# Letting the weights stand and the tokens move in the gate, up, gated-convolution and second query/key projections

## What is computed

```
# first block
h = rms_norm(x, attn_norm);  x = x + mixer1(h) @ w_out
h = rms_norm(x, ffn_norm);   x = x + (silu(h @ w_gate) * (h @ w_up)) @ w_down          # 2048 -> 5632 -> 2048
# second block; sh, sc, g come from silu(c) @ ada_w + ada_b
h = rms_norm(x, mix_pre_g) * (1 + sc1) + sh1
proj = h @ w_in                       # q, k, v (8 heads of 128 each), a, g (1024 each)
u = conv(a * sigmoid(g));  u = silu(layer_norm(u))                 # depthwise, 31 taps
y = concat(attention(q, k, v), u) @ w_out;   x = x + g1 * rms_norm(y, mix_post_g)
h = rms_norm(x, ffn_pre_g) * (1 + sc2) + sh2
y = (silu(h @ w_gate) * (h @ w_up)) @ w_down;   x = x + g2 * rms_norm(y, ffn_post_g)
```

## Time and profile before

| | |
|---|---|
| median of 3 runs | 2319.97 us (2319.22 to 2321.0) |
| the profiled execution | 2319.94 us |
| its span | 2318.0 us |
| TensorE busy, weight loads busy | 98%, 81% of the span |
| VectorE, ScalarE, GpSimd busy | 65%, 47%, 8% |
| HBM | 508.04 MB read, 220 GB/s over the span |

### The profile page before, as it was taken

How to read it: one execution, slowest core, us unless ns; L and a number is a source line. 1 busy time by engine, 2 the same in 40 slices (tenths; PEclk the granted TensorE clock), 3 DMA queues, 4 the chain that set the end, 5 groups by cost and what they waited for, 6 DMA issues and landing times.

```text
span 2318.0 us, 29331 instructions
## 1 busy us (share of the span) xinstructions
PE 2264.0 (98%) x10348; PEld 1870.6 (81%) x10348; DVE 1516.0 (65%) x1956; ACT 1086.5 (47%) x1515; POOL 174.3 (8%) x194
## 2 busy tenths in 40 slices
PE   8999999999999999999999999989999999999998
PEld 6888877888888888888878887777888888888886
DVE  5445476767777777777776886776777544554545
ACT  5565453544434444344445775544443344444444
POOL 5000100000000000000001885000000000000000
PEclk9999999999999999999999999999999999999999
DMA  7556507678888888888766664575888666666654
GB/s 222 177 177 195 160 28 278 228 254 283 276 280 282 279 276 277 288 279 276 260 228 191 192 185 122 210 262 180 278 276 269 190 190 189 191 190 195 190 179 150
DMA packets 274503, 511.79 MB, mean 221 GB/s; under 512 B 20071, under 2 KB 28949, under 8 KB 274124
## 3 DMA queue, kind: packets, MB, share of 16 engines
q1 hardware_dynamic: 270252, 509.94, 69.4%
q10 hardware_dynamic: 4128, 0.26, 0.1%
HBM read 508.04 MB, written 2.10 MB: 220 GB/s over the span
## 4 chain that ended last, share of the span: by engine, by line
PE 93%; DVE 2%; issue 1%; ACT 1%; DMA 1%; SPq 0%; DVEq 0%; ACTq 0%
PE bank L945 30%; PE bank L961 28%; PE bank L962 28%; DMA raw<-in_w_out 1%; PE bank L916 1%; PE bank L1018 1%; PE bank L1090 1%; PE bank L930 1%; PE bank L1006 1%; ACT w_hi L1381 0%; DVE ada_acc L1770 0%; PE bank L1059 0%; PE bank L818 0%; PE bank L1047 0%; PE bank L1009 0%
## 5 line engine op out<-in xcount | busy, mean ns | idle before, releaser
L1793 DVE TENSOR_TENSOR w_lo<-raw,w_hi 128x1024 fp32r<-128x1024 f32 x760 | 936.9, 1236 | 598.8 <-ACT w_hi L1381 591.2
L1381 ACT ACTIVATE w_hi<-raw 128x1024 fp32r<-128x1024 f32 x760 | 802.3, 1059 | 976.3 <-PE bank L945 930.4
L961 PE MATMUL bank<-w_hi,act_hi 128*128 128x512 f32 x2016 | 793.2, 393 | 3.6 <-DVE act_lo L1583 3.6
L962 PE MATMUL bank<-w_hi,act_lo 128*128 128x512 f32 x2016 | 786.5, 390 | 0.0
L945 PE MATMUL bank<-w_lo,act_hi 128*128 128x512 f32 x2080 | 558.1, 390 | 0.0
L945 PEld LDWEIGHTS bank<-w_lo,act_hi 128*128 128x128 f32 x2080 | 391.5, 188 | 82.5
L961 PEld LDWEIGHTS bank<-w_hi,act_hi 128*128 128x128 f32 x2016 | 379.6, 188 | 82.2 <-DVE act_lo L1583 4.2
L962 PEld LDWEIGHTS bank<-w_hi,act_lo 128*128 128x128 f32 x2016 | 379.7, 188 | 78.0 <-issue 0.7
L961 PE MATMUL bank<-w_hi,mid_hi 128*128 128x512 f32 x960 | 380.1, 396 | 11.8 <-ACT w_hi L1381 8.6
L962 PE MATMUL bank<-w_hi,mid_lo 128*128 128x512 f32 x960 | 375.4, 391 | 0.0
L1770 DVE SCALAR_TENSOR_TENSOR ada_acc<-ada_raw,c_act,ada_acc 128x512 f32<-128x512 f32 x360 | 269.7, 749 | 7.7 <-DMA ada_raw<-in_ada_w 0.5
(11 more groups left out here) (269 smaller groups left out, 1009.1 us busy)
## 6 DMA issues: line engine op xcount, KB each, us to landing
ada_raw<-in_ada_w SPq DMA_DIRECT2D x192, 512.0 KB, 5.2
raw<-in_w_gate SPq DMA_DIRECT2D x176, 512.0 KB, 4.4
raw<-in_w_up SPq DMA_DIRECT2D x176, 512.0 KB, 4.5
raw<-in_w_down SPq DMA_DIRECT2D x176, 512.0 KB, 4.4
raw<-in_w_in SPq DMA_DIRECT2D x168, 512.0 KB, 3.9
raw<-in_w_out SPq DMA_DIRECT2D x64, 512.0 KB, 5.5
raw<-in_cmp_w_k SPq DMA_DIRECT2D x4, 512.0 KB, 4.5
raw<-in_cmp_w_v SPq DMA_DIRECT2D x4, 512.0 KB, 4.5
```

Of the source, the lines that this page charges most:

```text
L961: pe.matmul(A_[t][:, :], h_, w_hi[:, s, kk, :], start=(k == 0), stop=False)
L962: pe.matmul(A_[t][:, :], l_, w_hi[:, s, kk, :], start=False, stop=False)
L1381: act.activation(w_hi[:, U % SPLIT_SLOTS].rearrange("p k n -> p (k n)"), raw[:, R % RAW_SLOTS].rearrange("p k n -> p (k n)"), ACT.Copy).th ...
L1793: dve.tensor_tensor(w_lo[:, U % SPLIT_SLOTS].rearrange("p k n -> p (k n)"), raw[:, R % RAW_SLOTS].rearrange("p k n -> p (k n)"), w_hi[:, U ...
```

## The change

For gate and up of both feed-forwards, and in the second input projection for a, g, queries and keys (the kinds `gate`, `up`, `keep_a`, `glu` and the `plain` ones of the second block; `across(C)` says which), a block of 128 rows by 128 weight columns is the stationary operand and the 256 tokens move. The result comes out turned, so the transposes and the copies behind them go. A unit becomes eight row blocks by 128 columns, except in the first chunk of a stage (`WHOLE`), which keeps the shape of the old unit because its inputs arrive block by block; its banks are first cleared with a product by zero. Tokens now lie along the free dimension, so the reciprocal root of the first feed-forward's norm can no longer be a scale per partition: it is spread to all partitions by one product (`rs_row`), VectorE multiplies the gate by it before Silu, and for up it is left out and applied where the down result is added to x. `mid_hi` and `mid_lo` are made from `zsb`. The value projections, the first stage, output and down chunks stay as they were.

```diff
+    WHOLE = (S_FFN1[0]["C"], S_IN2[0]["C"], S_FFN2[0]["C"])
+    KH = KPU * CW // P
...
-    TURNS = [c for _, c in IN1 if c[0] != "value"] + [c for _, c in IN2 if c[0] not in ("value", "keep_a")]
+    TURNS = [c for _, c in IN1 if c[0] != "value"]
+    DIRECT = [c for _, c in IN2 if c[0] == "plain"]
+    ACROSS = ("gate", "up", "keep_a", "glu")
+    def across(C):
+        p = consumer_of[C]
+        return p[0] in ACROSS or p in DIRECT
...
+                    if across(c["C"]) and c["C"] not in WHOLE:
+                        k, n0 = KH * (u % 2), at(c["n0"] + P * (u // 2), r, c["n_step"])
+                        sp.dma_start(raw[:, R % RAW_SLOTS].rearrange("p a n -> p (a n)").rearrange(
+                            "p (k n) -> p k n", n=P), W[c["w"]][:, k:k + KH, bass.ds(n0, P)]).then_inc(
+                            raw_loaded[R % RAW_SLOTS], 16)
...
-                if prev[0] == "up":
-                    q = prev[1]
-                    pe.wait_ge(h_ready, at(2 * q + 2, r, 2))
-                    if q >= 1:
-                        pe.wait_ge(mid_lo_done, at(2 * q, r, 2))
-                    for t in range(TT):
-                        for c in range(HPC):
-                            ins = pe.transpose(TURN[t][:, c * P:(c + 1) * P], zsb[:, t, c * P:(c + 1) * P], ident[:, :])
-                        ins.then_inc(h_turned, 1)
...
+                if across(c["C"]):
+                    whole = c["C"] in WHOLE
+                    part_of = list(itertools.product(range(KPU), range(HPC))) if whole else list(range(KH))
+                    def block(m, a, w, stop=False):
+                        if whole:
+                            kk, j = m
+                            k, lhsT = KPU * u + kk, w[:, s, kk, j * P:(j + 1) * P]
+                        else:
+                            j, k = u // 2, KH * (u % 2) + m
+                            lhsT = w[:, s].rearrange("p k n -> p (k n)")[:, m * P:(m + 1) * P]
+                        return pe.matmul(A_[j // 2][:, j % 2 * T:(j % 2 + 1) * T], lhsT, a[:, k, :],
+                                         start=(not whole and k == 0 and a is hi and w is w_hi),
+                                         stop=(stop and k == KD - 1 and not (whole and j % 2 == 0)))
+                    pe.wait_ge(hi_done, at(U + 1, r, 2 * nu))
+                    if whole and u == 0:
+                        pe.wait_ge(zero_made, 1)
+                        for b in range(2):
+                            pe.matmul(A_[b][:, :], w_hi[:, s, 0, 0:P], zero[:, 0:1].to_broadcast([P, CW]), start=True,
+                                      stop=False)
...
+                    for m in part_of:
+                        block(m, hi, w_hi)
+                        block(m, lo, w_hi)
+                    pe.wait_ge(lo_done, at(U + 1, r, 2 * nu))
+                    for m in part_of:
+                        ins = block(m, hi, w_lo, stop=True)
+                    return ins
...
+                if u == 6:
+                    pe.wait_ge(diag_made, 1)
+                    pe.matmul(MISC[1][:, 0:T], ones[:, :], zsb[:, 0, 0:T], start=True, stop=True).then_inc(
+                        rs_spread, 1)
...
-                    for t in range(TT):
-                        g = rstd[:, 1, t:t + 1] if q < FF // CW else 1.0
-                        act.activation(ysb[:, t, :], A_[t][:, :], ACT.Silu, scale=g).then_inc(sig_ready, 1)
+                    for b in range(2):
+                        if q < FF // CW:
+                            act.wait_ge(gate_scaled, at(2 * q + b + 1, r, 2))
+                        act.activation(ysb[:, b, :], ysb[:, b, :] if q < FF // CW else A_[b][:, :],
+                                       ACT.Silu).then_inc(sig_ready, 1)
...
+                elif prev in DIRECT:
+                    for b in range(2):
+                        h0 = prev[2] + 2 * b
+                        ins = act.activation(heads[prev[1]][:, h0:h0 + 2, :].rearrange("p h t -> p (h t)"), A_[b][:, :],
+                                             ACT.Copy, scale=-SCALE if prev[1] == "mq" else 1.0)
...
+                    if q < FF // CW:
+                        for b in range(2):
+                            dve.tensor_tensor(ysb[:, b, :].rearrange("p (j t) -> p j t", t=T),
+                                              A_[b][:, :].rearrange("p (j t) -> p j t", t=T),
+                                              rs_row[:, :].unsqueeze(1).to_broadcast([P, 2, T]),
+                                              ALU.mult).then_inc(gate_scaled, 1)
...
+                        elif dst == "x" and C > S_FFN1[0]["C"]:
+                            ins = dve.scalar_tensor_tensor(o, A_[t][:, :], rstd[:, 1, t:t + 1], o, ALU.mult, ALU.add)
```

More of the change, by code:

```diff
@@ L295, in build_two_blocks @@
         if p[0] in ("gate", "up", "glu"):
-            READ[C] = (p[0], 2 * p[1] + 2)
+            READ[C] = (("gate1" if p[0] == "gate" and p[1] < FF // CW else p[0]), 2 * p[1] + 2)
         else:
@@ L446, in build_two_blocks @@
         Cs.close()
+        Es = ExitStack()
+        rs_row = sb("rs_row", [P, T], F32, Es)
+        Es.close()
         Ds = ExitStack()
@@ L752, in _ @@
             pool.wait_ge(lf_d, 2)
-            pool.wait_ge(turned, len([c for _, c in IN1 if c[0] != "value"]))
+            pool.wait_ge(turned, len(TURNS))
             for j in range(FOX_H):
@@ L938, in products @@
                 n = HEADS.index(c["C"]) + 2 if c["C"] in HEADS else None
+                if across(c["C"]):
[5 more added lines that the diff above has]
+                            k, lhsT = KPU * u + kk, w[:, s, kk, j * P:(j + 1) * P]
+                        else:
+                            j, k = u // 2, KH * (u % 2) + m
[9 more added lines that the diff above has]
+                                      stop=False)
+                    if n is not None:
+                        for m in part_of:
+                            block(m, hi, w_hi)
+                        pe.wait_ge(lo_done, U + 1)
+                        for m in part_of:
+                            block(m, hi, w_lo)
+                        pe.wait_ge(act_lo_done, n * NU + u + 1)
+                        for m in part_of:
+                            ins = block(m, lo, w_hi, stop=True)
+                        return ins
+                    for m in part_of:
+                        block(m, hi, w_hi)
+                        block(m, lo, w_hi)
+                    pe.wait_ge(lo_done, at(U + 1, r, 2 * nu))
+                    for m in part_of:
+                        ins = block(m, hi, w_lo, stop=True)
+                    return ins
                 def part(a, w, stop=False):
@@ L1348, in post @@
                     return
-                if prev[0] == "up":
-                    q = prev[1]
-                    k0 = at(prev[2], r, 4)
-                    for t in range(TT):
-                        act.wait_ge(h_turned, at(2 * q + t + 1, r, 2))
-                        act.activation(mid_hi[:, bass.ds(k0, 4), t * P:(t + 1) * P],
-                                       TURN[t][:, :].rearrange("p (k t) -> p k t", t=P), ACT.Copy).then_inc(
-                            mid_hi_done, 1)
+                if prev not in TURNS:
                     return
@@ L1387, in split @@
                         pre(c["prev"], c["C"], r)
+                    if u == 4 and c["prev"] and c["prev"][0] == "up":
+                        up_hi(c["prev"], r)
                     if c is S_IN1[SMALL_OUT] and u == 6:
@@ L1649, in after @@
                         mean_root(1)
+                        for t in range(TT):
+                            ins = dve.tensor_scalar(zsb[:, 0, t * P:(t + 1) * P], ident[:, :], rstd[:, 1, t:t + 1],
+                                                    None, ALU.mult)
+                        ins.then_inc(diag_made, 1)
                 split(c, None, after=after)
@@ L1719, in post @@
                     return
-                if prev[0] == "up":
-                    q = prev[1]
-                    k0 = at(prev[2], r, 4)
-                    for t in range(TT):
-                        dve.wait_ge(mid_hi_done, at(2 * q + t + 1, r, 2))
-                        dve.tensor_tensor(mid_lo[:, bass.ds(k0, 4), t * P:(t + 1) * P],
-                                          TURN[t][:, :].rearrange("p (k t) -> p k t", t=P),
-                                          mid_hi[:, bass.ds(k0, 4), t * P:(t + 1) * P].bitcast(F32),
-                                          ALU.subtract).then_inc(mid_lo_done, 1)
+                if prev not in TURNS:
                     return
@@ L1731, in post, with up_lo @@
                 keep(dve, prev, 1, lambda o, s, g: dve.tensor_scalar(o, s, g, None, ALU.mult), turn_out_d)
+            def up_lo(prev, r):
+                q, k0 = prev[1], at(prev[2], r, 4)
+                for b in range(2):
+                    dve.wait_ge(mid_hi_done, at(2 * q + b + 1, r, 2))
```

(8 more changed lines are left out.)

103 lines of the change are left out of this document (53 added, 50 removed).

## The result

The changed kernel takes 2360.78 us, the median of four runs (2358.36 to 2363.44), against 2319.59 of the kernel before (2318.31 to 2321.0). The ratio is 1.018, its 95% interval 1.0168 to 1.0192: **41 us slower**. The profiled execution has a span of 2356.6 us.

What follows compares the result with a forecast made beforehand. The prediction took TensorE's own pace to bound the kernel. From 2319.94 us, -25.2 for transposes, +21.6 for 256-column multiplies and +1.8 for small additions gave 2318.1, say 2318 us; range 2292 to 2384.

Steps and rivals of the forecast that it cites:

- the first rival: Changed TensorE units: each weight change costs extra, 0.122 us per 256-column multiply, +84 us, 2381 us in all; chance 0.25.
- I take p = 0.1155, between the start-to-start reading and this floor: Gate, up and second input projection: p, the pace of a 256-column multiply, is 0.1155 us, so a unit takes 2.772 us.
- the term +21.6: Cost in us of 24 multiplies of 256 columns replacing 12 of 512, 0.052 more per unit over 416 units.
- The two readings of the earlier trace: Small projection, kernel before: 256-column multiply pace read as 0.115 us from start to start, 0.122 over the whole unit.
- a tail shed once per group: Small projection: 512-column multiplies behind short instructions start 0.23 us apart, not 0.227, an extra paid once per short group.
- the steady pace is the short step: Changed TensorE units: 256-column multiplies take 0.113 us, a unit 2.71 us, total 2293 us; faster rival, chance 0.23.
- The transposes: Gated unit, gated convolution input, second queries and keys: removing 28 groups at 0.90 us each saves 25.2 us.
- The floor of the loads: TensorE weight loads: 32 loads with nearly nothing to multiply take 3.72 us, so loads alone set 0.116 us each.
- the "much faster" rival: Changed TensorE units: a 256-column multiply costs its columns alone, 0.109 us, giving 2253 us; chance 0.02.
- The Silu behind the scaled gate: First feed-forward: ScalarE's Silu waits some 2 us for VectorE, hidden by a lead of 8 us, costed at nothing.
- The 512-byte pieces: Changed weight loads: 1024 pieces of 512 B replace 256 of 2 KB, DMA share 0.92, costed at nothing.
- the DMA rival: Gate-and-up loads: scattered small pieces make DMA engines the bound, 13 pairs +37 us, 2355 us; chance 0.08.

Runs made afterwards that it cites:

- the experiment with 1.8 of a shorter wait in it: The kernel before without its 28 groups of eight transposes, output not the reference's: 2291.07 us, ratio 0.9886.
- the second experiment: The kernel before with each 512-column multiply of gate, up and second input projection made as two of 256, transposes kept: 2382.47 us, ratio 1.0281.

## Why the prediction was right or wrong

**The sign and size.** The forecast of 2318, no change, was wrong by 43 us, though the time lies inside the range of 2292 to 2384. The chances had 0.43 on slower and 0.37 on faster, so the way it went was the likeliest of the three, and the single number hid that. What came is the first rival, "each change of weights has a price of its own", with the 0.120 of its own argument rather than the 0.122 of its sum.

**The step that failed** is "I take p = 0.1155, between the start-to-start reading and this floor", and with it the term +21.6, which measured +66.6 in the changed kernel (2.88 per unit) and +64 where the splitting was tried by itself (400 units). Two things went wrong in it. The record it was read from has 64 columns standing; the steady pace of that shape is 0.1133, that of 128 columns 0.120, and the forecast asked only whether the wider load could hide, against a floor of 0.116, instead of whether it adds to the columns. And the argument for the true value stood in the text: 0.227 is 0.013 over the columns alone. It was set back because plain float32 records take 0.216. The bfloat16 kernels have 0.2158 at 512 columns and 0.1092 at 256, while the rounded 32-bit type has 0.2267 and 0.120: the charge goes with the type, and a record of another type says nothing of it. What in the engine makes it 0.0133, and 0.0067 behind 64 columns, stays open.

**The two readings of the earlier trace rows.** Neither the starts (0.115) nor the unit account (0.122) gave the steady pace of 0.1133. Four short instructions among long ones are too few; that the ends of the group blur both is my reading, not tested. The reasoning about a tail shed once per group was right, and "the steady pace is the short step" was right for that shape. It was the wrong shape.

**The transposes.** -25.2 forecast, -25.5 by the trace before, and 26.4 to 27.3 in the experiment with 1.8 of a shorter wait in it. Right. That TensorE waited 3.1 us for mid_lo, and that this would go, was not in the sum.

**The floor of the loads.** 0.116 forecast, 0.112 measured with 192 columns moving, and 0.112 in the earlier trace rows too when read from start to start: the forecast took the whole piece, with its tail, and divided by 32. The floor was too low to be what sets 0.120. The Trainium skill (Perfetto Trace Analysis, Identifying the Most-Contended Engine) judges TensorE by its share of time in weight loads, and the sign came out its way: 81% to 90%, and 99.5 to 100% in the changed chunks. But a share near 100% did not mean that loads could come no faster: in the 192-column experiment the same load, still shown as 0.19 us, came every 0.112, so at 0.120 they had room. The shown busy time of loads overlaps itself. The loads still have a part in the price, since behind 64 columns the same multiply takes 0.1133.

**TensorE's table.** The Trainium skill (TensorE: Matmul & The Clock Gate, Back-to-back issue gap) has 518 cycles for 512 columns and 262 for 256, 0.216 and 0.109 us at 2.4 GHz. The bfloat16 kernels here agree (0.2158, 0.1092). The kernel of this case, in the rounded 32-bit type, does not (0.2267, 0.120), and the chance of the "much faster" rival was rightly small.

**What was costed at nothing.** The Silu behind the scaled gate: 11 waits of up to 1.9 us, 20 in all, none passed on to TensorE. The copies to mid_hi and mid_lo: no wait of TensorE for them in the down chunks. The 512-byte pieces: some 1 us, DMA share 0.88 to 0.90 where 0.92 was forecast, no wait for a gate or up load; the DMA rival did not happen. Down units kept 2.72 us. That the late down load would cost some 3 us more was not foreseen.

## What to carry to other kernels

Count the multiplies as well as their columns: halving the moved width doubles the number of times that the charge per multiply is paid. Here it is 0.0133 us in the rounded 32-bit type and 0.0025 in bfloat16, so the same rearrangement loses in one type and wins in the other. Read that charge from start to start in a steady run of the exact shape, type and stationary width. If the kernel has none, split its long multiplies and measure that, as the second experiment does; failing this, say that the row is of another shape and give the rule fitted to the long multiplies (columns plus a constant) more weight. And a change made of two nearly equal terms of opposite sign is decided by the smaller doubt: here 0.005 us on a price that is paid 9984 times.

## What the runs showed of the hardware

- A multiply in the rounded 32-bit type behind a load of 128 standing columns takes 0.120, 0.1733 and 0.2267 us for 256, 384 and 512 moved columns: the columns at 2.4 GHz and 0.0133 us. With 192 columns it takes 0.112 and not 0.093; plain float32 multiplies of 32 columns behind such loads take 0.112 too.
- With 256 moved columns the pace is 0.118, 0.1133, 0.116 and 0.120 for 32, 64, 96 and 128 standing ones. The order is not understood.
- bfloat16 takes 0.1092 and 0.2158 for 256 and 512 columns when its operands are contiguous, and 0.1133 for 256 when they are read 4 bytes apart.
- Eight 128x128 transposes between two units add 0.91 us.
- Behind an idle time of 2.16 us of TensorE the granted clock of the next 6 us was 0.72 in the changed kernel, and 1.00 behind 2.15 us in the kernel with 2 KB pieces.
